# 1/rms applied to finished products, and the residual update spread over three engines, in a two-layer hybrid decoder

## What is computed

```python
def _rms_norm(x, g):
    y = x * rsqrt(mean(x * x, axis=-1) + 1e-6)
    return y * g
def _modulated_norm(x, g, shift, scale):
    return _rms_norm(x, g) * (1.0 + scale) + shift
def _swiglu(h, w_in, w_out):
    gate, up = split(h @ w_in, 2)
    return (silu(gate) * up) @ w_out
# per layer; mod = silu(c) @ ada_w + ada_b, nine rows of 1024
h = _modulated_norm(x, g0, shift0, scale0);  x = x + 0.5 * gate0 * _swiglu(h, ...)
h = _modulated_norm(x, g1, shift1, scale1);  x = x + gate1 * token_mixer(h, ...)
h = _modulated_norm(x, g2, shift2, scale2);  x = x + 0.5 * gate2 * _swiglu(h, ...)
```

## Time and profile before

| | |
|---|---|
| device time, median of 3 runs | 1379.89 us (1378.99 to 1381.31) |
| span of the profiled execution | 1372.7 us |
| time of the profiled execution itself | not listed apart; the median stands 7.2 us above the span |
| TensorE busy | 95% of the span |
| VectorE, ScalarE, GpSimd busy | 68%, 46%, 18% |
| mean granted TensorE clock | 0.989 |
| read from HBM | 295.6 MB |

### The profile page before, as it was taken

The page is one execution under the profiler, slowest core; times in us unless marked ns, Lnnn a source line. Parts: engine busy times, 40 slices in busy tenths (PEclk is TensorE's granted clock), DMA queues, the critical chain, the costliest instruction groups (busy, mean ns, idle before and its releaser), DMA issues.

```text
span 1372.7 us, 30033 instructions
## 1 busy us (share of the span) xinstructions
PE 1306.4 (95%) x12978; PEld 1268.2 (92%) x12978; DVE 933.1 (68%) x1324; ACT 631.5 (46%) x907; POOL 240.8 (18%) x265
## 2 busy tenths in 40 slices
PE   2999999999899999999999999999999999999998
PEld 1999999988799989999999999998878999999997
DVE  6777678666756776666676776766765478667655
ACT  2543435566524455443354433537563344543443
POOL 1233430001020001332013331100103000123300
PEclk9999999999999999999999999999999999999999
DMA  9988975515103746776768887662430175577762
GB/s 360 356 294 281 316 281 194 215 47 215 63 4 145 300 162 240 276 289 231 280 229 291 292 310 264 245 246 65 180 124 4 65 288 186 199 262 297 276 222 95
DMA packets 65136, 298.25 MB, mean 217 GB/s; under 512 B 9217, under 2 KB 10241, under 8 KB 47746
## 3 DMA queue, kind: packets, MB, share of 16 engines
q1 hardware_dynamic: 65026, 296.69, 59.2%
HBM read 295.62 MB, written 1.05 MB: 216 GB/s over the span
## 4 chain that ended last, share of the span: by engine, by line
PE 84%; DVE 9%; ACT 3%; DMA 2%; issue 1%; DVEq 1%; SPq 0%; ACTq 0%; POOL 0%; POOLq 0%
PE PS L1419 23%; PE PS L1420 23%; PE PS L1421 23%; PE PS L1825 3%; DVE wl L868 3%; PE PS L1491 1%; PE PS L1431 1%; PE PS L1643 1%; PE PS L1433 1%; PE PS L1437 1%; DMA raw<-in_ada_w 1%; DVE scr L894 1%; DMA raw<-in_branch_w 1%; DVE raw L954 1%; DMA ada_w_ring<-in_ada_w 1%
## 5 line engine op out<-in xcount | busy, mean ns | idle before, releaser
L868 DVE TENSOR_TENSOR wl<-raw,wh 128x1024 fp32r<-128x1024 f32 (+1 forms) x400 | 470.5, 1216 | 291.9 <-ACT wh L547 291.9
L547 ACT ACTIVATE wh<-raw 128x1024 fp32r<-128x1024 f32 (+1 forms) x400 | 396.8, 1039 | 479.4 <-PE PS L1421 428.8
L1419 PE MATMUL PS<-h_hi,wh 128*128 128x256 f32 x2160 | 602.8, 279 | 9.0 <-DVE wl L868 4.8
L1420 PE MATMUL PS<-h_lo,wh 128*128 128x256 f32 x2160 | 598.0, 277 | 0.0
L1421 PE MATMUL PS<-h_hi,wl 128*128 128x256 f32 x2160 | 597.9, 277 | 0.0
L1419 PEld LDWEIGHTS PS<-h_hi,wh 128*128 128x128 f32 x2160 | 406.1, 188 | 14.1 <-issue 10.3
L1420 PEld LDWEIGHTS PS<-h_lo,wh 128*128 128x128 f32 x2160 | 405.9, 188 | 0.2
L1421 PEld LDWEIGHTS PS<-h_hi,wl 128*128 128x128 f32 x2160 | 405.8, 188 | 0.0
L954 DVE SCALAR_TENSOR_TENSOR ada_w_ring<-ada_w_ring,c_row 128x1024 f32<-128x1024 f32 x154 | 186.8, 1218 | 11.2 <-ACT c_row L608 7.0
L1421 PE MATMUL PS<-hid_hi,wl 128*128 128x256 f32 x704 | 194.3, 276 | 0.0
L1419 PE MATMUL PS<-hid_hi,wh 128*128 128x256 f32 x704 | 194.3, 276 | 0.0
(11 more groups left out here) (283 smaller groups left out, 1426.6 us busy)
## 6 DMA issues: line engine op xcount, KB each, us to landing
raw<-in_ffn_w_in SPq DMA_DIRECT2D x88, 1024.0 KB, 5.5
ada_w_ring<-in_ada_w SPq DMA_DIRECT2D x154, 512.0 KB, 5.1
raw<-in_mix_w_in SPq DMA_DIRECT2D x46, 1024.0 KB, 5.7
raw<-in_ffn_w_out SPq DMA_DIRECT2D x44, 1024.0 KB, 5.8
raw<-in_branch_w SPq DMA_DIRECT2D x8, 1024.0 KB, 10.7
raw<-in_mix_w_out SPq DMA_DIRECT2D x8, 1024.0 KB, 4.8
raw<-in_ada_w SPq DMA_DIRECT2D x6, 512.0 KB, 10.8
raw<-in_mix_w_in SPq DMA_DIRECT2D x4, 512.0 KB, 3.6
```

The lines of the kernel that those rows point to most:

```text
L547: nc.scalar.activation(wh[:, s % 2, h * n:(h + 1) * n], raw[:, s % 4, h * n:(h + 1) * n], ACT.Copy).then_inc(*one("w_hi"))
L868: V.tensor_tensor(wl[:, s % 2, h * n:(h + 1) * n], raw[:, s % 4, h * n:(h + 1) * n], wh[:, s % 2, h * n:(h + 1) * n].bitcast(F32), ALU.sub ...
L1419: M(out, wh[(slice(None),) + wsl], rhs_h, start=start, stop=False, skip_group_check=True)
L1420: M(out, wh[(slice(None),) + wsl], rhs_l, start=False, stop=False, skip_group_check=True)
```

## The change

The norm is linear in x but for the factor 1/rms of each token, so (x * g * (1 + scale) / rms + shift) @ W = (x * g * (1 + scale)) @ W / rms + shift @ W. The changed kernel forms u = x * g * (1 + scale) without waiting for the root, with the shift as further columns (two equal ones, so a product has 258 columns), and multiplies the finished product with 1/rms.

- **Who makes what.** ScalarE makes `uh` (high part of u) from x directly, VectorE `ul`. The output blocks 0, 1, 4, 5 and 7 are added to x on VectorE; for 2, 3 and 6 ScalarE multiplies with the gate (`gated`) and GpSimd adds (`x_blocks`). Squares, their sum and the root come after the first slot of the new sub-layer; GpSimd adds all eight squares, so that TensorE sums one block (4 rows of 1 column) in place of five.
- **FFN slots.** A slot's two halves no longer fit one bank, and take two (`glu_banks`); two slots then share four banks, and slot j waits until an earlier slot's `sil` is there (`glu_freed`). VectorE multiplies both halves with 1/rms out of PSUM (`glu_scale`), ScalarE copies the shift columns and does Silu with the shift as bias (`glu_gate`), VectorE adds the other shift and multiplies (`glu_out`). At a seam this starts only in loop step 1, when `keep_rms` has been done.
- **Mixer.** Slots 33 to 35 are done with u and scaled afterwards on VectorE (`qk_scale`), shifted on ScalarE. From slot 36 on h is used as before; it is now made by ScalarE (x * g * (1 + scale)), GpSimd (times 1/rms), ScalarE (plus shift, `hh`) and VectorE (`h_lo`). Slot 36 takes its products block by block.
- The SP queue's code is not touched.

```diff
+UT = T + 2
...
+def glu_banks(f, j):
+    if j == 2:
+        return (5, 6)
+    if j < 2:
+        return ((0, 1), (2, 3))[(f + j) % 2]
+    return ((2, 3), (0, 1))[j % 2]
+def glu_freed(f, j):
+    return (1 + f, 2)[j - 3] if j < 5 else j - 1
...
+            def keep_rms(l, n, inc=one):
+                act.wait_ge(*at("rb_done", n, l))
+                nc.scalar.activation(rms, rms_row(n), ACT.Copy).then_inc(*inc("rms_ready"))
+            def gated(l, n, c):
+                gc = (n - 1) * KD + c
+                act.wait_ge(*at("out_done", 4 * (n - 1) + BLOCK_DONE[c], l))
+                nc.scalar.activation(scr[:, c, :], out_block(n - 1, c), ACT.Copy, scale=gatec[:, gc:gc + 1])\
+                    .then_inc(*one("xt_ready"))
...
+            def u_hi(l, n, c):
+                if n:
+                    x_done(l, n, c)
+                nc.scalar.activation(uh[:, c, 0:T], x[:, c, :], ACT.Copy, scale=gsc[:, n % 3, c:c + 1])\
+                    .then_inc(*one("uh_ready"))
+            def between(l, n, s, ls):
+                act.wait_ge(*at("out_done", 4 * (n - 1) + 1, l))
+                u_shift(l, n)
+                gated(l, n, 2)
+                gated(l, n, 3)
+                for c in range(4):
+                    u_hi(l, n, c)
+                gated(l, n, 6)
+                for c in range(4, KD):
+                    u_hi(l, n, c)
+                round_w(s + 1, still, ls)
+                squares(l, n)
+            def glu_gate(l, f, j):
+                q = j % 2
+                act.wait_ge(*at("tg_ready", f * KF + j + 1, l))
+                nc.scalar.activation(shift_cols[:, q, :], pair(glu_banks(f, j), T, T + 1).rearrange("p a b -> p (a b)"),
+                                     ACT.Copy)
+                act.drain()
+                act.wait_ge(*at("hf_ready", f * KF + j - 1, l))
+                nc.scalar.activation(sil[:, q, :], tg[:, q, 0, :], ACT.Silu, bias=shift_cols[:, q, 0:1])\
+                    .then_inc(*one("sil_ready"))
...
+                late = l or f
+                for j in range(KF):
+                    s = s0 + j
+                    act.wait_ge(*loaded(s + 2, still, l))
+                    act.wait_ge(*at("w_used", s + 1, l))
+                    round_half(s + 2, 0, still, l)
+                    if j == 1 and late:
+                        keep_rms(l, 2 * f)
+                    if j > 1 or not late:
+                        glu_gate(l, f, j)
+                    round_half(s + 2, 1, still, l)
+                    if j == 0 and late:
+                        root(l, 2 * f)
+                        nc.scalar.activation(warm_silu[:, :], one_b[:, :], ACT.Silu)
+                    if j == 1 and late:
+                        glu_gate(l, f, 0)
+                        glu_gate(l, f, 1)
...
+                round_w(ATT_IN + 2, still, l)
+                for c in range(KD):
+                    nc.scalar.activation(xg[:, c, :], x[:, c, :], ACT.Copy, scale=gsc[:, 1, c:c + 1])\
+                        .then_inc(*one("xg_ready"))
+                root(l, 1)
+                act.wait_ge(*loaded(SLOT_V, still, l))
+                act.wait_ge(*at("w_used", SLOT_V - 1, l))
+                round_half(SLOT_V, 0, still, l)
+                keep_rms(l, 1)
...
+            def u_lo(l, n, c):
...
+                V.scalar_tensor_tensor(ul[:, c, 0:T], x[:, c, :], gsc[:, n % 3, c:c + 1], uh[:, c, 0:T].bitcast(F32),
+                                       ALU.mult, ALU.subtract).then_inc(*one("ul_ready"))
+            def between(l, n, s, ls):
+                split_half(s, 0, still, ls)
+                x_block(l, n, 0)
+                x_block(l, n, 1)
+                split_half(s, 1, still, ls)
+                u_lo(l, n, 0)
+                u_lo(l, n, 1)
+                x_block(l, n, 4)
+                x_block(l, n, 5)
+                u_lo(l, n, 2)
+                x_block(l, n, 7)
+                for c in range(3, KD):
+                    u_lo(l, n, c)
+                split(s + 1, still, ls)
+            def glu_scale(l, f, j):
+                dve.wait_ge(*at("w_used", (FFN1_IN, FFN2_IN)[f] + j + 1, l))
+                if j == 0:
+                    dve.wait_ge(*at("rms_ready", 2 * f, l))
+                if j > 1:
+                    dve.wait_ge(*at("hf_ready", f * KF + j - 1, l))
+                V.tensor_tensor(tg[:, j % 2], pair(glu_banks(f, j), 0, T), rms2, ALU.mult).then_inc(*one("tg_ready"))
+            def glu_out(l, f, j):
+                dve.wait_ge(*at("sil_ready", f * KF + j + 1, l))
+                dve.wait_ge(*at("hid_ready", f * KF + j - 1, l))
+                V.scalar_tensor_tensor(hf[:, j % 2, :], tg[:, j % 2, 1, :], shift_cols[:, j % 2, 1:2], sil[:, j % 2, :],
+                                       ALU.add, ALU.mult).then_inc(*one("hf_ready"))
...
-                for s, o in steps(dve, s0, KF, *((0, 0), (4, 2))[f]):
-                    j = s - s0
-                    split(s + 2, o, l)
-                    dve.wait_ge(*at("sil_ready", f * KF + j + 1 + o(4), l))
-                    dve.wait_ge(*at("hid_ready", f * KF + j - 1 + o(4), l))
-                    V.tensor_tensor(hf[:, j % 2, :], PS[:, j % 4, T:2 * T], sil[:, j % 2, :], ALU.mult)\
-                        .then_inc(*one("hf_ready"))
+                late = l or f
+                for j in range(KF):
+                    s = s0 + j
+                    if j > 1 or not late:
+                        glu_scale(l, f, j)
+                        split_half(s + 2, 0, still, l)
+                        glu_out(l, f, j)
+                        split_half(s + 2, 1, still, l)
+                    else:
+                        split(s + 2, still, l)
+                    if j == 0 and late:
+                        norm_root(l, 2 * f)
+                    if j == 1 and late:
+                        for v in range(2):
+                            glu_scale(l, f, v)
+                        for v in range(2):
+                            glu_out(l, f, v)
                     if f == 0 or 4 <= j < 20:
-                        ada((16, 60)[f] + j, o, l)
+                        ada((16, 60)[f] + j, still, l)
...
+                    V.tensor_copy(shift_cols[:, i, :], pair(ATT_BANKS[i], T, T + 1).rearrange("p a b -> p (a b)"))
+                    V.tensor_tensor(qk[:, 2 * i:2 * i + 2, :], pair(ATT_BANKS[i], 0, T), rms2, ALU.mult)\
+                        .then_inc(*one("qk_scaled"))
...
+                ada(46, still, l)
+                split(ATT_IN + 2, still, l)
                 norm_root(l, 1)
-                norm(l, 1)
-                split(ATT_IN + 1, still, l)
-                ada(46, still, l)
+                split_half(SLOT_V, 0, still, l)
+                qk_scale(0)
+                qk_scale(1)
+                split_half(SLOT_V, 1, still, l)
+                for c in range(4):
+                    h_lo(c)
+                split_half(SLOT_V + 1, 0, still, l)
+                h_lo(4)
+                qk_scale(2)
+                h_lo(5)
+                split_half(SLOT_V + 1, 1, still, l)
+                h_lo(6)
+                h_lo(7)
                 ada(47, still, l)
-                for s in range(ATT_IN, RW_IN - 1):
-                    split(s + 2, still, l)
-                    ada(48 + s - ATT_IN, still, l)
+                for s in range(SLOT_V + 2, RW_IN + 1):
+                    split(s, still, l)
+                    ada(48 + 2 * (s - SLOT_V - 2), still, l)
+                    ada(49 + 2 * (s - SLOT_V - 2), still, l)
...
+            def x_blocks(l, n):
+                for i, c in enumerate(POOL_BLOCKS):
+                    pool.wait_ge(*at("xt_ready", 3 * (n - 1) + i + 1, l))
+                    G.tensor_tensor(x[:, c, :], x[:, c, :], scr[:, c, :], ALU.add).then_inc(*one("xp_ready"))
...
-                for s, o in steps(pe, s0, KF, peel=(2, 6)[f]):
+                for s, o in steps(pe, s0, KF, peel=6):
                     j = s - s0
-                    pe.wait_ge(*at("hf_ready", f * KF + j - 3 + o(4), l))
+                    banks = glu_banks(f, j)
+                    if j > 2:
+                        pe.wait_ge(*at("sil_ready", f * KF + glu_freed(f, j) + o(4), l))
                     if j == 0:
-                        ins = first_slot(s, 0, f * 2 * KD, l)
+                        ins = u_first(s, banks, f * 2, l)
                     for half in range(2) if j else ():
                         split_ready(s, half, o, l)
-                        ins = in_tile(s, half, j % 4, half * T)
+                        ins = u_tile(s, half, banks[half])
+                        if j == 2 and half == 0 and (l or f):
+                            norm_rows(l, 2 * f)
                     ins.then_inc(*one("w_used"))
+                    if j == 1 and (l or f):
+                        norm_sums(l, 2 * f, (0,))
...
+                u_first(ATT_IN, ATT_BANKS[0], 1, l).then_inc(*one("w_used"))
+                for half in range(2):
```

(10 more changed lines are left out.)

288 lines of the change are left out of this document (170 added, 118 removed).

## The result

The changed kernel takes 1438.33 us, median of 4 runs (1437.65 to 1440.54), against 1380.60 (1378.99 to 1386.52) for the kernel before: a ratio of 1.044 with a 95% interval of 1.039 to 1.048. The forecast was 1379.0, at most 1392; the change costs 58 us.

A forecast was written before the change was run, and what follows sets the result against it. TensorE, busy for 95% of the span, was taken to bound the kernel. FFN seams -12.9, mixer seams +8.2, end +2.2, start -0.4, columns 0 and pace +2 sum to -0.9, giving 1379.0 us, range 1367 to 1392.

The forecast's parts named there:

- Two columns more: In 4512 products, 258 columns in place of 256 cost 0 us, bounds 0 to +4.0.
- The clock: In mixer seams, lower clock level after the stall before slot 39: 1.9 us at half a chance, 1.0 a seam.
- GpSimd at 0.76 an addition: At the seams, seven GpSimd additions of squares at 0.76 us, the last ending at about T+10.7, so sums do not wait.
- FFN seams: At three FFN seams, the loss falls from 21.2 to 8.3 us with the first slot starting at T: -12.9 us.
- Mixer seams: At two mixer seams, loads held behind ada 47 stall slots 38 and 39; each loses 10.8 for 6.7 us: +8.2 us.
- the loads come in time: Rival, chance 0.18: in mixer seams slots 38 and 39 stall less than half as long; 1362.6 to about 1371 us.
- The pace after a stall: New stalls inside FFNs can start products at 0.118 us in place of 0.1133: +2 us, bounds 0 and +22.
- The end: At the kernel's end, later squares and GpSimd's later sum bring the root at T+4.5 in place of T+2.3: +2.2 us.
- the columns that are paid: Rival, chance 0.12: the two further columns of the products cost 4.0 us, giving 1383.0 us.
- the bound of the FFN slots: Rival, chance 0.04: VectorE needs over 5.44 us an FFN slot, 4.5 worked out; over 1388 us.
- The base: The profiled span of 1372.7 us plus 7.2 us lying around it, which the change leaves alone.

The follow-up runs named there:

- e1: The changed kernel with 256 columns in place of 258 in each product on u, leaving out the shift term: 1409.23 us.
- e5: The changed kernel with half slots of FFN slots 6 to 21 given widths from 128 to 320 columns, to measure ns per product: 1444.11 us.
- e10: The kernel before, with three more GpSimd additions of 128x256 in each slot from slot 6 of FFN 1 of layer 0: 1388.98 us, one run.
- e7: e6 with GpSimd adding only three times at every seam, as before the change, and TensorE summing five blocks: 1406.04 us.
- e4: The changed kernel with VectorE's ada 47 of the mixer seams moved to right behind the split of slot 35, 48 to 53 one place earlier: 1416.67 us.
- e2: The changed kernel with 272 columns in place of 258 (sixteen equal shift columns, two of them read): 1452.54 us, one run.
- e6: e4 with the residual of all eight blocks on VectorE, as before the change; GpSimd still adds all eight squares: 1412.35 us.

## Why the prediction was wrong

**Two columns more, 0 with bounds 0 to +4.0: the step that failed most.** It measured +31.5 in the account and 29.1 by e1, over seven times the upper bound. The prediction argued from one-column products of 0.12 us that columns do not set the pace, so two more are free, and bounded the cost in proportion. The reading of that row was off: 2.40 us run to the modelled end of the last product. From start to start the source view of that line has (221.2 - 219.1) / 19 = 0.11 us a product:

```profile
L1491 PE MATMUL PS<-cst,scr x20: 164/250/271, 219.1 to 221.2; 128*128 128x1 f32 x20
```

So one column costs slightly less than 256, not more, and as much as 128 or 224 (111.6 ns). The argument was near the truth for narrow products, but it tells nothing about the step at 256, where the pace lies 1.7 ns above the floor and any other width near it 5 to 7 higher. A floor under narrow products is no evidence that the width in use can grow. The kernel before has streams of such products at 256 columns and, in slot 37, at 128 alone, and e5 is the measurement that the step lacked.

The Trainium skill (TensorE: Matmul & The Clock Gate, section Back-to-back issue gap) gives by its formula for an isolated stream an estimate of 109.2 and 110.0 ns for 256 and 258 columns; measured are 113.3 and 120.0. The same page of the Trainium skill, section LDWEIGHTS, gives for a load of 128 columns of weights an estimate of 128 / 1.2 = 106.7 ns, and Back-to-back issue gap says that load and product set the spacing together; the floor of 111.6 ns in e5, the same from 128 to 224 columns, fits a limit of that kind, 4.9 ns above the figure. None of them has the favoured 256.

**The clock, 1.0 a mixer seam and nothing in an FFN: failed in its size.** The prediction let all of the seams' loss of before go, stretches at the half level included, and put 2.0 us in all for new ones in the mixers. The changed kernel has 187 product steps at the half level up to the fifth slots and the 577th products, about 19 us, where before had 100, about 10. The half level came after the wait for the sums or for the fourth slot in every FFN seam, and in the mixer seams after each of the three longest waits, not at half a chance.

**GpSimd at 0.76 an addition: failed in its price.** Squares ended at T+7.65 (232.40), forecast +7.4: right. The additions took 1.33 each, not 0.76, because in the earlier trace rows VectorE stood beside them on PSUM, and now it splits weights. The sum was 4.5 us late in the mixer seams and 3.0 in the FFN seams (it ends at T+13.7 there), hence "slot 2 ends at +10.9, so the sums go in without a wait" was wrong by 1.5 to 2.9 us at every seam. The Trainium skill (GPSIMD Engine Reference, section Key points) says that GpSimd shares its SBUF interfaces with VectorE and contends with VectorE's instructions that have two SBUF inputs. e10 agrees, 0.73 against 1.70 us; the prediction had no term for it.

**FFN seams, -12.9: measured -0.9.** The first slot at T and the scaling at 0.68 (measured 0.69) were right. So was the wait ahead of the fourth slot in size, forecast 1.6 with f=0 and 2.3 with f=1: TensorE is idle for 1.17, and for 1.79 twice. In time it was not: the fourth slot starts at T+22.3 to +23.7, forecast +18.7 to +19.4, both sides of that wait being late. Missing in the loss (20.3 us in place of 8.3) were the waits for the sums, 1.5 us each, the stretches at the half level (78 steps, about 7 us) and the waits inside the first slot, about 0.4 each. In e7, with the wait for the sums gone, the fifth slot still comes at +29.9, +28.0 and +29.9.

**Mixer seams, +8.2: measured +27.2.** The mechanism was right, the queue held by ada 47 behind the last low part, with slot 38 issued together with ada 51. ada 47 is done at +31.8 in place of +25.3, since the root is late and the split and the low parts beside GpSimd take 1.76 and 0.90 in place of 1.14 and 0.40. But TensorE was late too, so the stalls ahead of slots 38 and 39 came out as forecast in sum: 4.37 + 3.44 and 2.81 + 3.56 = 14.2 us, forecast 14.4 (2.05 and 5.15 in each seam; that the sum fits is partly luck). What was too small is the rest: the clock, 109 steps or about 11 us in place of 2.0, the waits for the sums, 2.94 and 2.88 in place of 0, the low parts in slot 36, and 0.7 in each first slot. e4 shows that moving one ada step takes both stalls away, with the clock behind them 21.7 us: the rival "the loads come in time" would have needed exactly that edit.

**The pace after a stall, +2: right in size.** One output stage of FFN 2 ran at 117.8 ns, +2.3. That it was one is luck: how many output stages run so differs from run to run, none in e1, four in e2. **The end, +2.2:** measured +3.5. The forecast had two of its causes, later squares (TensorE idle for 1.41 us) and a later sum by GpSimd (0.46); the clock was missing, the last one-column products stand 0.213 us apart. In e6, where VectorE adds all blocks again, the end is as short as before. **The rivals:** the one that came about is the columns that are paid, given 0.12 and priced at 4.0. VectorE did not become the bound of the FFN slots, with 68.19 of 80 us busy, but a slot cost it 4.9 us, not 4.5; in e1, at the pace of 256 columns, it is busy for 76.62 of 80, close to the bound. The loads were not in time, but later.

**The base.** The prediction took the 7.2 us between span and median for time around the program. Where a run's span is listed they are 1.8 apart (1374.0 and 1372.2); the profiled execution of before was simply among the shorter ones. This cancels in the forecast, but not in the size of a difference of spans.

## What to carry to other kernels

Before a width is changed on the engine that bounds the kernel, measure the pace at the new width; proportion is no bound, and here 250 and 258 columns were both 6% slower than 256. An operation's price belongs to its neighbours too: take it from a row in which the other engine does what it will do after the change. Where a queue holds loads for two users, look for the one step of the slower user on which the next load of the other hangs; moving it was worth 22 us here, a quarter of that from the clock. Idle time taken from one place does not free the clock if other waits of TensorE follow.
